# A two-block transformer kernel on one core: the hybrid layers' output projection computed by token tiles, with the norms behind it taken per token row

## The reference, cut to what matters

```
def hybrid_layer(x, pos, g_pre, w_in, ..., g_grp, w_out, g_post):
    h = rmsnorm_2(x, g_pre) @ w_in
    (a_q, a_k, a_v, b_b, b_c, b_x, c_q, c_kv, c_kr, d_q, d_k, d_v, gate) = jnp.split(h, SPLIT_IDX, axis=-1)
    ...                                   # ya, yb, yc, yd: four mixers of width 256
    y = jnp.stack([ya, yb, yc, yd], axis=2)
    y = rmsnorm_2(y, g_grp.reshape(N_GROUPS, GROUP_WIDTH)).reshape(b, s, D_MIX)
    y = y * jax.nn.silu(gate)
    return x + rmsnorm_2(y @ w_out, g_post)
```

## Time and profile before

| what | value |
|---|---|
| median of 3 runs (lowest, highest) | 3000.63 us (2996.49, 3001.14) |
| profiled execution, its own time | 2999.35 us |
| span of its trace | 2997.6 us |
| TensorE busy | 2915.8 us, 97% |
| VectorE, ScalarE busy | 1446.1 us, 998.0 us |
| mean granted TensorE clock | 0.983 |

### The profile page before, as it was taken

The page is one execution under the profiler, slowest core; times in us unless marked ns, Lnnn a source line. Parts: engine busy times, 40 slices in busy tenths (PEclk is TensorE's granted clock), DMA queues, the critical chain, the costliest instruction groups (busy, mean ns, idle before and its releaser), DMA issues.

```text
span 2997.6 us, 36777 instructions
## 1 busy us (share of the span) xinstructions
PE 2915.8 (97%) x13442; PEld 2386.8 (80%) x13442; DVE 1446.1 (48%) x2087; ACT 998.0 (33%) x1546; POOL 0.2 (0%) x4
## 2 busy tenths in 40 slices
PE   8999999999999999999999999999998999999996
PEld 6888888788888887888887778888887777777775
DVE  6443346545544425443355554554425554455555
ACT  3222224333322313222123333232223344434453
POOL 0000000000000000000000000000000000000000
PEclk9999999999999999999999999999999998999998
DMA  4333232212233322333232212233332211122111
GB/s 141 98 93 103 84 117 78 71 49 91 92 101 95 105 91 92 97 93 104 84 117 85 70 43 91 85 102 94 98 105 78 71 51 48 50 78 71 43 42 57
DMA packets 69368, 251.67 MB, mean 84 GB/s; under 512 B 7696, under 2 KB 7824, under 8 KB 69008
## 3 DMA queue, kind: packets, MB, share of 16 engines
q1 hardware_dynamic: 68400, 246.46, 26.4%
q10 hardware_dynamic: 864, 3.79, 0.3%
HBM read 248.13 MB, written 2.10 MB: 83 GB/s over the span
## 4 chain that ended last, share of the span: by engine, by line
PE 92%; DVE 4%; ACT 2%; issue 1%; DMA 0%; DVEq 0%; SPq 0%; ACTq 0%
PE bank L476 25%; PE bank L478 25%; PE bank L477 25%; PE bank L584 1%; PE bank L585 1%; PE bank L586 1%; PE bank L639 1%; PE bank L649 1%; PE bank L829 1%; PE bank L815 1%; PE bank L840 1%; PE bank L706 1%; PE bank L759 1%; PE bank L786 1%; PE bank L771 1%
## 5 line engine op out<-in xcount | busy, mean ns | idle before, releaser
L476 PE MATMUL bank<-xh,wh 128*128 128x512 f32 x2384 | 943.8, 396 | 16.4 <-DVE start_d L2082 9.2
L478 PE MATMUL bank<-xh,wl 128*128 128x512 f32 x2384 | 932.1, 391 | 0.0
L477 PE MATMUL bank<-xl,wh 128*128 128x512 f32 x2384 | 932.0, 391 | 0.0
L1472 DVE TENSOR_TENSOR wl<-raw,wh 128x1024 fp32r<-128x1024 f32 x460 | 561.4, 1221 | 300.7 <-ACT wh L1079 300.0
L1079 ACT ACTIVATE wh<-raw 128x1024 fp32r<-128x1024 f32 x460 | 483.0, 1051 | 393.5 <-PE bank L478 247.5
L476 PEld LDWEIGHTS bank<-xh,wh 128*128 128x128 f32 x2384 | 450.5, 189 | 114.5 <-issue 18.5
L478 PEld LDWEIGHTS bank<-xh,wl 128*128 128x128 f32 x2384 | 450.0, 189 | 95.1
L477 PEld LDWEIGHTS bank<-xl,wh 128*128 128x128 f32 x2384 | 450.5, 189 | 93.0 <-issue 1.9
L476 PE MATMUL bank<-uh,wh 128*128 (+1 forms) x704 | 273.9, 389 | 0.0
L477 PE MATMUL bank<-ul,wh 128*128 (+1 forms) x704 | 273.9, 389 | 0.0
L478 PE MATMUL bank<-uh,wl 128*128 (+1 forms) x704 | 273.9, 389 | 0.0
(11 more groups left out here) (355 smaller groups left out, 2850.2 us busy)
## 6 DMA issues: line engine op xcount, KB each, us to landing
raw<-stream SPq DMA_DIRECT2D x460, 512.0 KB, 3.5
x<-x_t SPq DMA_DIRECT2D x4, 512.0 KB, 7.0
dec<-decay ACTq DMA_DIRECT2D x2, 1024.0 KB, 6.0
out<-x SPq DMA_DIRECT2D x8, 256.0 KB, 2.0
rp<-rope ACTq DMA_DIRECT2D x2, 512.0 KB, 6.5
cst<-const SPq DMA_DIRECT2D x1, 708.5 KB, 10.1
ffraw<-ff_w ACTq DMA_DIRECT2D x2, 316.0 KB, 10.2
posi<-pos SPq DMA_DIRECT2D x1, 256.0 KB, 10.3
```

What stands on the lines that cost most here:

```text
L476: pe.matmul(o, wh[:, s, c], rhs_h, start=first, stop=False)
L477: pe.matmul(o, wh[:, s, c], rhs_l, start=False, stop=False)
L478: return pe.matmul(o, wl[:, s, c], rhs_h, start=False, stop=last)
L1472: dve.tensor_tensor(wl[:, at.slot, :], raw[:, at.raw, :], wh[:, at.slot, :].bitcast(F32), ALU.subtract).then_inc(split_lo, 1)
```

## The change

In both hybrid layers the output projection takes the gated operand as stationary (128 tokens) and weight columns as moving (`by_token`); the panels of `w_out` are laid out anew for it. A first half makes output columns 0 to 511 for all four token tiles at once (banks 4 to 7), gated tile by gated tile in the order `READY`; a second half makes columns 512 to 1023, token tile by token tile (banks 0 to 3). The result is token-major, so ScalarE gets the sum of squares of a token row from `accum_out` in a `Square`, and VectorE applies 1/rms as a value per partition; gains per feature come as rows broadcast over partitions (`g_post`, `g_next`, 512 KB each), loaded from ScalarE's queue. The residual needs x token-major: in layer 0 TensorE turns x in eight batches between the sliding-window heads (`turn_x`), and ScalarE copies them to `xt`. After layer 0 each token tile is normed with the next layer's pre norm and gain (`next_normed`), turned (`turn_next`), split (`next_high`, `next_low`), and the next layer's token-major stage runs token tile by token tile; its one-column sums, its norm chain and its products with 1/rms are gone (plain copies instead). After layer 1 no operands are made, and four stores of 512 KB take the place of eight of 256 KB. Some buffers and banks move; `cxs` shares `diag`.

```diff
-        FILL_BANK = (0, 1, 0, 1, 0, 1, 0, 1, 7, 7, 7, 7, 7, 2)
+        FILL_BANK = (0, 1, 0, 1, 0, 1, 0, 1, 7, 7, 7, 7, 7, 6)
...
-        GROUP_BANKS = ((3, 4), (0, 1), (5, 6))
-        OUT_BANKS = (7, 2)
+        GROUP_BANKS = ((4, 5), (0, 1), (2, 3))
+        OUT_BANKS = ((4, 5, 6, 7), (0, 1, 2, 3))
+        X_TURNED = ((0, 1, 2), (3, 4, 5), (6, None, 7))
...
+            for t in range(TT):
+                sp.wait_ge(*post.at((DEPTH - 1) * TT + t, "X"))
+                sp.dma_start(out[t], x[:, 2 * t:2 * t + 2, :]).then_inc(stored, 16)
...
+                def turn_x(batch):
+                    if m or batch is None:
+                        return
+                    t, c = batch // 2, batch % 2
+                    if batch == 0:
+                        pe.wait_ge(*resid.at((FINAL + 1) * KD + KD - 1, "X"))
+                    else:
+                        pe.wait_ge(*x_tok.at(batch - 1, "E"))
+                    for i in range(KD // 2):
+                        last = pe.transpose(bank[4][:, i * P:(i + 1) * P],
+                                            x[:, c * (KD // 2) + i, t * P:(t + 1) * P], ident)
+                    last.then_inc(x_tr.sem, 1)
...
-                token_major(q0 + BT_TM, (4, 5, 6, 7), TM_COLS, lambda k: pe.wait_ge(*hyb_xl.at(m * KD + k, "XL")),
-                            after_tile=sum_squares)
+                if m == 0:
+                    token_major(q0 + BT_TM, (4, 5, 6, 7), TM_COLS, lambda k: pe.wait_ge(*hyb_xl.at(k, "XL")),
+                                after_tile=sum_squares)
                 col_panel(bank[2][:], q0 + BT_CQ)
-                chain_bc(n, 1)
+                if m == 0:
+                    chain_bc(n, 1)
...
                     fill(m, MH + h)
+                    turn_x(batches[0])
                     pe.wait_ge(*swa_ex.at(it, "X"))
                     swa_turn(m, h)
                     if h < SWH - 1:
                         swa_scores(m, h + 1)
                     else:
+                        if m == 0:
+                            pe.wait_ge(*x_tok.at(2 * TT - 1, "E"))
                         stick_scores(m, 0)
+                    turn_x(batches[1])
 
                     pe.wait_ge(*(swa_dve.at(it - 1, "O") if h else mla_dve.at(m * MH + MH - 1, "O")))
                     swa_values(m, h)
+                    turn_x(batches[2])
...
-                pe.wait_ge(*gn.at(m, "DG"))
-                pe.wait_ge(*gate_y.at(m * KD + 1, "Y"))
-                pe.matmul(bank[3][:], ones, diag[:], start=True, stop=True).then_inc(gn_pe.sem, 1)
...
+                def by_token(o, t, k, yh, yl, at, c, first, last):
+                    tok = slice(t * P, (t + 1) * P)
+                    pe.matmul(o, yh[:, k, tok], wh[:, at.slot, c], start=first, stop=False)
+                    pe.matmul(o, yl[:, k, tok], wh[:, at.slot, c], start=False, stop=False)
+                    return pe.matmul(o, yh[:, k, tok], wl[:, at.slot, c], start=False, stop=last)
+                w0 = q0 + BT_WOUT
+                pe.wait_ge(*gate_in.at(m * KD + KD - 1, "G"))
+                for j, k in enumerate(READY):
+                    at, c = w0 + j // 2, slice(j % 2 * S, (j % 2 + 1) * S)
+                    if j % 2 == 0:
+                        panel_ready(at)
+                    pe.wait_ge(*gate_l.at(m * KD + j, "L"))
+                    for t in range(TT):
+                        last = by_token(bank[OUT_BANKS[0][t]][:], t, k, ygh, ygl, at, c, j == 0, j == KD - 1)
+                    if j % 2 == 1:
+                        last.then_inc(panel_done, 1)
+                    if j == 1:
+                        pe.wait_ge(*gn.at(m, "DG"))
+                        pe.wait_ge(*gate_y.at(m * KD + 2, "Y"))
+                        pe.matmul(bank[0][:], ones, diag[:], start=True, stop=True).then_inc(gn_pe.sem, 1)
+                pe.wait_ge(*gn.at(m, "B1"))
+                pe.wait_ge(*gate_y.at(m * KD + 5, "Y"))
+                def turn_next(t):
+                    pe.wait_ge(*next_h.at(t, "H"))
+                    for c in range(2):
+                        for i in range(KD // 2):
+                            d = c * (KD // 2) + i
+                            last = pe.transpose(bank[OUT_BANKS[c][t]][:, i * P:(i + 1) * P],
+                                                hn[:, t % 2, d * P:(d + 1) * P], ident)
+                    last.then_inc(next_tr.sem, 1)
+                for t in range(TT):
                     for j, k in enumerate(READY):
+                        at, c = w0 + KD // 2 + j // 2, slice(j % 2 * S, (j % 2 + 1) * S)
+                        if t == 0 and j % 2 == 0:
+                            panel_ready(at)
+                        last = by_token(bank[OUT_BANKS[1][t]][:], t, k, ygh, ygl, at, c, j == 0, j == KD - 1)
+                        if t == TT - 1 and j % 2 == 1:
+                            last.then_inc(panel_done, 1)
+                        if m < DEPTH - 1 and t >= 2 and j == KD // 2 - 1:
+                            turn_next(t - 2)
+                    if t < TT - 1:
+                        last.then_inc(out_pe.sem, 1)
+                if m == DEPTH - 1:
+                    return
+                first, rest = range(KD // 2), range(KD // 2, KD)
+                for t, tiles, turned in ((0, first, 2), (1, first, None), (0, rest, None), (1, rest, 3),
+                                         (2, range(KD), None), (3, range(KD), None)):
+                    pe.wait_ge(*next_lo.at(t, "B"))
+                    for k in tiles:
+                        at = q0 + LAYER2 + k // 2
+                        panel_ready(at)
+                        c = slice(k % 2 * S, k % 2 * S + TM_COLS)
+                        last = by_token(bank[4 + t][:, 0:TM_COLS], t, k, xh, xl, at, c, k == 0, k == KD - 1)
+                        if t == TT - 1 and k % 2 == 1:
+                            last.then_inc(panel_done, 1)
+                    if turned:
+                        turn_next(turned)
...
+                def x_turned(batch):
+                    if m or batch is None:
+                        return
+                    act.wait_ge(*x_tr.at(batch, "T"))
+                    act.activation(xt[:, batch, :], bank[4][:], ACT.Copy).then_inc(x_tok.sem, 1)
...
-                    if d == KD - 2:
+                    if d == 3:
                         gate_hi(0)
                         gate_hi(1)
...
+                act.dma_start(g_post[:], rows[2 * m]).then_inc(rows_in, 16)
+                if m < DEPTH - 1:
+                    act.dma_start(g_next[:], rows[2 * m + 1]).then_inc(rows_in, 16)
+                ahead(BT_WOUT, KD // 2 + 1)
+                act.wait_ge(panel_done, (q0 + BT_WOUT).done(KD // 2))
+                for t in range(TT):
+                    last = act.activation(gates[:, t, :], bank[OUT_BANKS[0][t]][:], ACT.Square,
+                                          accum_out=zsum[:, 0, t:t + 1])
+                last.then_inc(out_sq.sem, 1)
                 act.wait_ge(sqrt_set, m + (DEPTH + 1))
...
+                def out_std(t):
+                    if t < TT - 1:
+                        act.wait_ge(*out_pe.at(m, f"T{t}"))
+                    else:
+                        act.wait_ge(panel_done, (q0 + BT_WOUT).done(KD))
+                    act.activation(gates[:, TT + t, :], bank[OUT_BANKS[1][t]][:], ACT.Square,
+                                   accum_out=zsum[:, 1, t:t + 1]).then_inc(out_sq.sem, 1)
+                    act.wait_ge(*out_rest.at(m, "B"))
+                    act.wait_ge(*out_sq.at(m, f"Q{t}"))
+                    act.activation(zstd[:, t:t + 1], zsum[:, 1, t:t + 1], ACT.Sqrt, bias=zrest[:, t:t + 1],
+                                   scale=1.0 / D).then_inc(out_sd.sem, 1)
+                def next_std(t):
+                    act.wait_ge(*post.at(m * TT + t, "X"))
+                    squares = slice(t % 2 * 2, t % 2 * 2 + 2)
+                    act.activation(gates[:, squares, :].rearrange("p a s -> p (a s)"),
+                                   x[:, 2 * t:2 * t + 2, :].rearrange("p a s -> p (a s)"), ACT.Square,
+                                   accum_out=xsum[:, t:t + 1]).then_inc(next_sq.sem, 1)
+                    act.wait_ge(*next_sq.at(t, "Q"))
+                    act.activation(xstd[:, t:t + 1], xsum[:, t:t + 1], ACT.Sqrt, bias=eps[:], scale=1.0 / D)\
+                       .then_inc(next_sq.sem, 1)
+                def next_high(t):
+                    act.wait_ge(*next_tr.at(t, "T"))
+                    for c in range(2):
+                        act.activation(xh[:, c * (KD // 2):(c + 1) * (KD // 2), t * P:(t + 1) * P],
+                                       bank[OUT_BANKS[c][t]][:].rearrange("p (d c) -> p d c", c=P), ACT.Copy)\
+                           .then_inc(next_hi.sem, 1)
+                if m == DEPTH - 1:
+                    for t in range(TT):
+                        out_std(t)
+                    return
+                out_std(0)
+                next_std(0)
```

(78 more changed lines are left out.)

195 lines of the change are left out of this document (95 added, 100 removed).

## The result

The changed kernel took 2959.26 us (median of 4 runs, 2954.33 to 2964.51), the kernel before, on the same chip, 3000.89 us (2996.49 to 3001.61): a ratio of 0.9861, 95% interval 0.9847 to 0.9875. That is 41.6 us less, where 32 were forecast. The profiled execution took 2962.62 us.

A forecast was written before the change was run, and what follows sets the result against it. TensorE, busy 97%, was taken as the bound, so gains come only where it waits, is slow-clocked or has finished. Gains 3.6, 12.2, 7.3, 16.0 less 4.1 and 3 give 32.0 us: 2969 us, range 2962 to 2980.

The forecast's parts named there:

- Out-projection, layer 0: Layer 0's output projection: 51.6 us before, 44.4 after, less 1.5 for delayed panels and 2.1 for two turns; gain 3.6 us.
- the 1.5 us for panel 7: Layer 0's projection: gain-row loads on ScalarE's queue delay the late weight panels; 1.5 us lost, bounds nothing to 3.5 us.
- Between the layers: From layer 0's last projection matmul to the second `cq` panel: 42.95 us before, 30.7 after, with 6.6 of waits; gain 12.2 us.
- `x` turned: Layer 0's sliding-window heads: 32 transposes at 0.129 us, all on TensorE's path; loss 4.1 us.
- Layer-1 projection: Layer 1's output projection: 52.2 us before, 44.4 after, less 0.5 for delay by gain-row loads; gain 7.3 us.
- The tail: After layer 1's last matmul: only one token tile left to norm and store; 23.7 us falls to 7.7, gain 16.0 us.
- The clock: Token-major stage or panel 7: short waits bring 1.2 GHz; loss from nothing to 8 us, 3 us taken.
- signs of being wrong: `hn` waits in token tiles three or four, mid-projection `wl` wait over 2 us, clock 0.50 over 15 us, layer-0 heads 6 us longer.
- Rival (b): Whole kernel: everything fits and the clock holds; gain 37 us and up to 2 more, 2962 to 2964 us; chance 0.12.
- Rival (c): Both projections: panel starvation, 3.5 us at panel 7 each, with the clock down; gain 22 us, 2979 us; chance 0.17.
- (d): Token-major stage: token tiles' chains do not overlap with panels, about 4 us more each, layer 0 gains nothing; 2984 us; chance 0.05.
- (e): Sliding-window stage and after: many 128-column transposes keep the clock at 1.2 GHz; slower than before; chance 0.03.

The follow-up runs named there:

- experiment 5: The changed kernel with two more 512 KB gain-row fetches, read by nobody, ahead of the two in layer 0: 2961.76 us, ratio 0.9872.
- late_gate: The changed kernel with the last gate product of a token tile row loaded after the third tile again, as before: 2968.38 us, ratio 0.9895.
- experiment 4: The changed kernel with only the earlier load of the last gate product undone: 2968.38 us, ratio 0.9895.
- experiment 3: The changed kernel with layer 0's transposes of x and their copies left out, 2957.88 us, or with each batch of transposes issued twice, 2964.03 us.

## Why the forecast was right in direction and low in size

By its own steps, forecast against the first pair of profiles:

- Out-projection, layer 0: forecast 3.6 us. From the first matmul to the end it took 2634.60 - 2588.26 = 46.3 us against 51.6 before: 5.3 us. The 192 matmuls, the broadcast and the two turns are right within 0.2 us; the 1.5 us for panel 7 is not there. This term was mis-sized, 0 measured. The forecast's own schedule, by which it just fits (ready 27.5 us behind the turn of `y_sb`), was right: 27.2 us, 0.6 us ahead of its use; the delay by the gain rows, added on top, was not (experiment 5). No wait for `ygl` is left with twelve uses of each gated tile, in late_gate neither, and the earlier load is worth 1.1 us a layer (experiment 4), which the forecast rightly counted at nothing lost. Of the 51.6 us up to 3.4 were falls of the clock.
- Between the layers: forecast 12.2 us, measured 42.95 - (2666.00 - 2634.60) = 11.6 us. The four waits are 4.8 us instead of 6.6, and one fall of the clock gave back 1.6 us (C is 24.33 us in the profile of the changed kernel without it, 25.9 in the two with it).
- `x` turned: forecast -4.1 us, measured -3.3 to -3.5 (experiment 3). The 0.129 us for a transpose was a duration divided by eight; start to start already had 2585.72 - 2584.84 = 0.88 us for eight, which gives 3.5 us.
- Layer-1 projection: forecast 7.3 us, measured 7.6: no wait for panel 7, against 0.5 counted. Up to 3.4 us of the time before were falls.
- The tail: forecast 16.0 us, measured 16.5. The store landed in 2.6 us. The forecast's estimate by the Trainium skill (DMA: Bandwidth & Descriptors, the two cost components) was 3.2 us for it, so the trace does not agree by 0.6 us; the page fits that formula to DMAs issued from GpSimd, and SyncE issues this one. The forecast's own 3.3 us around the store hold 2.8 us of landing, not the 2.6 that its sentence compares with.
- **The clock: forecast -3 us, bounds 0 to 8 of loss. This is the step that failed**, in sign. It asked only whether the new short waits would bring falls, and they brought one, of 1.6 us, in two profiles of three. It did not ask which falls go. Over B to E the falls sum to 15.3, 18.7 and 22.1 us in the kernel before, and to 5.1, 5.1 and 3.4 in the changed one; with A the means are 42.6 and 26.2 us, so that up to 16 of the 41.8 us are clock: 2.3 in A, 2.8 in B, 4.5 in C, 4.0 in D, 2.8 in E. What lies in B, C and E was in the sum unnamed, since their times before contained the falls and the new work was priced at 2.4 GHz. What lies in A and D was in no term: their work hardly changes (with the falls taken out D is 244.6 to 245.3 us before and 244.3 after), and the sum took D from the one profile of three without its large fall.

Without its clock term the sum was 35.0 us. To the 41.8 us between the means of three profiles, stage A adds 2.5 us (-1.6 instead of -4.1: 0.6 to 0.8 for the turns, 2.3 for the falls, and -0.6 from the start of the program, where profiles of the same kernel differ by 2.5 us), B 1.7, C and D together 2.6 (14.8 instead of 12.2), F 0.5, and E takes off 0.4.

Of the signs that it named as right, most came: no gap for `ygl`, 45.5 us from the turn of `y_sb` to the end of layer 1's projection, a last `x` 4.2 us after the last matmul, four waits for `wl`, the first of them 0.73 us, under its bound of 1; the transposes took 0.11 us, not 0.13. None of the signs of being wrong came. The mechanism of the change so stood as forecast, and the clock is what was off.

Rival (b), everything fits and the clock holds, was the nearest in mechanism with 2962 to 2964 us; it had 0.12 and its end became the range's. Rival (c) fell (no starvation), and (d) and (e) too: no wait for `hn` shows, and the window stage kept its clock. For (e) the forecast weighed a rule of the Trainium skill (TensorE: Matmul & The Clock Gate, PE-mode transpose), that transposes do not count as work for the clock. Neither 32 nor 64 of them between the heads showed what it would bring: those windows stand at 1.00, though the transposes stand in groups of four and eight among other matmuls there, so the runs don't settle the rule itself. Of the turns of `hn` one lies in the fall from 2638 to 2642 us, which began right behind the 1.36 us wait and ahead of the turn, the other three in none.

What stays open is what decides, at equal work and waits, whether the clock falls in D, and so how much of the 4.5 us there belongs to the change. The medians of the three groups with the changed kernel lie 41.6, 42.5 and 43.3 us apart, so the whole gain is steady; no run shows by what D takes part in it.
